# First projections of a three-block decoder: pairs of weight tiles by seven products instead of eight

## The chip, the cores and the metric

The kernel runs on one core of a Trainium2 chip. The metric is the device time of one execution in microseconds. The kernel before was timed three times: 2856.89, 2852.45 and 2854.75 us, median 2854.75.

## The reference, cut to what matters

The model is one block with three mixers side by side (window attention, RG-LRU, RWKV-7) and then two blocks with mixture-of-experts layers. Everything here happens at the very start of the first block, in the projection that makes the inputs of its three mixers:

```
D_MODEL = 1024; SEQ = 1024
proj = jnp.einsum("bsd,de->bse", x, w_in[l])                       # (1024 x 1024) @ (1024 x 2880), float32
q, k, v, g_a, x_b, g_b, c_cols, g_c = jnp.split(proj, split_idx, axis=-1)
y_a = _swa_sinks(q, k, v, attn_sinks[l])
y_b = _rg_lru(x_b, conv_w, conv_b, lru_wa, lru_ba, lru_wx, lru_bx, lru_lambda)   # conv, two sigmoid gates, scan
y_c, v_own = _rwkv7(c_cols, mu, w0, w2, a0, a2, k_k, k_a, r_k, gn_w, gn_b, vres) # token shift, tanh, sigmoids, state scan
y = jnp.concatenate([y_a * silu(g_a), y_b * silu(g_b), y_c * silu(g_c)], axis=-1)
```

## The kernel before, in words

`front` is the first phase of the program. It makes `proj` transposed: a tile is 128 output features (partitions) by 1024 tokens. `xT` holds x transposed, eight rows of 128 features by 1024 tokens (512 KB each). A tile's weights are 512 KB, loaded into one of two slots of `wbuf`. A tile is 16 matmuls of the source: two halves of 512 tokens, each a sum over eight rows of x (line 290). In float32 one matmul of the source shows as two instructions in the trace, so a tile is 32 instructions. `ORDER` is the order of the 20 tiles: two for the RG-LRU input (XB), one with the low-rank columns (WA), receptance (R), key (CK) and value (CV) of RWKV, two gates, four for the queries, one for the keys (K), four gates. Two more gate tiles (`LATE`) are made in the next phase. The attention values come with the tokens on the partitions and so are a separate group, `value_products` (line 270), 64 matmuls of 128 columns just ahead of the last tile.

The order of the work is written out by hand for each engine. TensorE goes through the tiles and puts six groups of `small` matmuls (line 245, four of the source each, 8 instructions) between them: two gate products of the RG-LRU, two low-rank products with only 32 rows, two sums over heads. ScalarE takes each tile out of PSUM in one piece (`evacuate`, line 299, the gates through Silu) and does the sigmoids, exponentials and roots of the mixers' inputs between them. VectorE does the convolution, the token shifts (`shift`, line 386), two scans, one reciprocal of 128x2048 (line 449) and products with it. SyncE loads tile m into a slot when tile m-2 is done. GpSimd issues the small loads, then makes masks, and has nothing more to do in this phase. The phase ends with a barrier of all engines. `acc` has four PSUM banks for the tiles, `aux` four for the small groups and the values.

The same way of seven products that the change brings in is already used two phases later, in `first_out` (`fo`, line 994): there GpSimd makes sums of operands (lines 1091 to 1096), TensorE runs groups of four matmuls (8 instructions, line 1110) and VectorE adds each product to its place (lines 1194 and 1201). Matrix shapes per group are the same: 128x128 weights by 128x512.

Of the kernel before, what the change touches and what calls it, by code (L numbers as in the profile page):

```python
# [11 lines left out]
P = 128  # L12
# [84 lines left out]
def col(v):  # L97
# [6 lines left out]
ORDER = [XB_T, XB_T + 1, WA_T, R_T, R_T + 1, CK_T, CK_T + 1, CV_T, CV_T + 1, G_T + 4, G_T + 5,  # L104
         Q_T, Q_T + 1, Q_T + 2, Q_T + 3, K_T, G_T, G_T + 1, G_T + 2, G_T + 3]
LATE = [G_T + 6, G_T + 7]
FRONT_TILES = len(ORDER)
K_AT = ORDER.index(K_T) + 1
GATE_AT = ORDER.index(G_T + 5) + 1


def in_tile(D, tile):
    return D["w_in_t"][tile - (tile > KS_T)]
# [22 lines left out]

def front(nc, D, proj, values, kkb, bb, dlt, wc, vec, win, ck):
# [5 lines left out]
    with Phase(nc, "fr") as ph:  # L143
        xT = win.xT
        wbuf = ph.sb("w", [P, 2, KT, P])
# [4 lines left out]
        keep = proj[:, KS_T]  # L150
        ones2 = ph.sb("ones2", [P, P])
# [7 lines left out]
        acc = ph.ps("acc", [P, 2, 2, 512])  # L159
# [4 lines left out]
        rr, kx, vv = (proj[:, m:m + TL] for m in (R_T, CK_T, CV_T))  # L164
        wv_loaded, loaded, vec_loaded = ph.sem("wv_loaded"), ph.sem("loaded"), ph.sem("vec_loaded")
        x_loaded = [ph.sem(f"x{k}_loaded") for k in range(KT)]
        w_loaded = [ph.sem("w0_loaded"), ph.sem("w1_loaded")]
        (done, evac, aux_done, aux_free, v_own, a_own, zeroed, conv_done, low_ready, tanh_low, sig_done, decay_done,
         tanh_done, root_in, root_done, logs_done, sq_ready, norm_done, cum_done, bonus_in, exp_done) = (ph.sem(n) for n in (
             "done", "evac", "aux_done", "aux_free", "v_own", "a_own", "zeroed", "conv_done", "low_ready", "tanh_low",  # L170
             "sig_done", "decay_done", "tanh_done", "root_in", "root_done", "logs_done", "sq_ready", "norm_done",
             "cum_done", "bonus_in", "exp_done"))
# [4 lines left out]

        with nc.Block() as block:

            @block.sync  # L180
            def _(sp):
                sp.dma_start(wbuf[:, 0], in_tile(D, ORDER[0])).then_inc(w_loaded[0], 16)
                for k in range(KT):
                    sp.dma_start(xT[:, k], D["xT"][:, k]).then_inc(x_loaded[k], 16)
                sp.dma_start(wbuf[:, 1], in_tile(D, ORDER[1])).then_inc(w_loaded[1], 16)
                for m in range(2, FRONT_TILES):

                    sp.wait_ge(done, m - 1)
                    sp.dma_start(wbuf[:, m % 2], in_tile(D, ORDER[m])).then_inc(w_loaded[m % 2], 16)
                    if m == FRONT_TILES - 1:  # L190

                        sp.wait_ge(evac, K_AT)
                        sp.wait_ge(cum_done, 1)
                        for h in range(2):
                            sp.dma_start(proj[HALF * h:HALF * h + HALF, KS_T],
                                         proj[HALF - HALF * h:P - HALF * h, K_T]).then_inc(turned_k, 16)
                for n, tile in enumerate(LATE):
                    sp.dma_start(win.wg[n], in_tile(D, tile)).then_inc(late_loaded, 16)
                sp.dma_start(win.sinks[:], D["attn_sinks"].partition_broadcast(P)).then_inc(late_loaded, 16)
                sp.wait_ge(turned_k, 32)  # L200
                sp.wait_ge(late_loaded, 48)

            @block.gpsimd
            def _(pool):
                pool.dma_start(lvec[:], D["lru_vec"]).then_inc(vec_loaded, 16)
# [3 lines left out]
                pool.dma_start(w2a2[RANK:2 * RANK], D["rwkv_a2"]).then_inc(loaded, 16)  # L209
                pool.wait_ge(zeroed, 1)  # L210
# [5 lines left out]
                pool.dma_start(wv, D["w_v_t"]).then_inc(wv_loaded, 16)  # L216
                g = nc.gpsimd
# [13 lines left out]
                for n in range(4):  # L231
                    select(ck.masks[:, n], ALU.is_ge if n % 2 == 0 else ALU.is_gt, -1, 1, 0.0, HALF)
                select(ck.lowm[:], ALU.is_ge, -1, 1, 1.0, HALF)
# [6 lines left out]
                select(ck.lowm[0:HALF], ALU.is_ge, -1, 1, 1.0)  # L240

            @block.tensor
            def _(pe):
                mm = nc.tensor.matmul
                def small(n, weights, moving, *waits):

                    if n:
                        pe.wait_ge(aux_free, n)
                    for s, value in waits:
                        pe.wait_ge(s, value)  # L250
                    for t in range(TL):
                        for c in range(2):
                            last = mm(aux[:, t, c], weights(t), moving(t)[:, 512 * c:512 * c + 512], start=True, stop=True)
                    last.then_inc(aux_done, 1)

                def smalls(m):
                    if m == 4:
                        small(0, lambda t: wa[:, t], lambda t: xc[:, t], (conv_done, 1), (loaded, 16 * 12))
                    if m == 5:
                        small(1, lambda t: wx[:, t], lambda t: xc[:, t])  # L260
                    if m == 10:
                        small(2, lambda t: w2a2[0:RANK, P * t:P * t + P], lambda t: lo[0:RANK], (tanh_low, 1))
                    if m == 11:
                        small(3, lambda t: w2a2[RANK:2 * RANK, P * t:P * t + P], lambda t: lo[RANK:2 * RANK])
                    if m == 14:
                        small(4, lambda t: ones2[:], lambda t: dlt[:, t], (sq_ready, 1))
                    if m == 16:
                        small(5, lambda t: ones2[:], lambda t: dlt[:, t], (bonus_in, 1))

                def value_products():  # L270
                    pe.wait_ge(wv_loaded, 16)
                    pe.wait_ge(aux_free, 6)
                    for t in range(NB):
                        for k in range(KT):
                            last = mm(aux[:, 0, t // 4, P * (t % 4):P * (t % 4) + P], xT[:, k, P * t:P * t + P], wv[:, k],
                                      start=(k == 0), stop=(k == KT - 1))
                    last.then_inc(aux_done, 1)

                for m in range(FRONT_TILES):
                    if m == FRONT_TILES - 1:  # L280
                        value_products()
                    b = m % 2
                    pe.wait_ge(w_loaded[b], 16 * (m // 2 + 1))
                    if m >= 2:
                        pe.wait_ge(evac, m - 1)
                    for c in range(2):
                        for k in range(KT):
                            if m == 0 and c == 0:
                                pe.wait_ge(x_loaded[k], 16)
                            last = mm(acc[:, b, c], wbuf[:, b, k], xT[:, k, 512 * c:512 * c + 512],  # L290
                                      start=(k == 0), stop=(k == KT - 1))
                    last.then_inc(done, 1)
                    smalls(m)

            @block.scalar
            def _(act):
                a = Chain(act, a_own)

                def evacuate(m):
                    act.wait_ge(done, m + 1)  # L300
                    gate = ORDER[m] < GATE_TILES
                    nc.scalar.activation(proj[:, ORDER[m]], flat(acc[:, m % 2]),
                                         ACT.Silu if gate else ACT.Copy).then_inc(evac, 1)
# [4 lines left out]
                for m in range(5):  # L308
                    evacuate(m)
                for n, (out, bias) in enumerate(((rg, 5), (ig, 6))):  # L310
                    act.wait_ge(aux_done, n + 1)
                    for t in range(TL):
                        a.hold(nc.scalar.activation(out[:, t], flat(aux[:, t]), ACT.Sigmoid, bias=lvec[:, t, bias:bias + 1]))
                    a.wait()
                    act.sem_inc(aux_free, 1)
                    evacuate(5 + n)
# [3 lines left out]
                act.sem_inc(tanh_low, 1)  # L320
                act.wait_ge(decay_done, 1)
# [4 lines left out]
                evacuate(7)  # L326
# [3 lines left out]
                for m in range(8, 11):  # L330
                    evacuate(m)
                for n, (out, bias) in enumerate(((lw, 3), (aa, 4))):

                    act.wait_ge(logs_done, 1)
                    act.wait_ge(aux_done, n + 3)
                    for t in range(TL):
                        a.hold(nc.scalar.activation(out[:, t], flat(aux[:, t]), ACT.Sigmoid, bias=vec[:, t, bias:bias + 1]))
                    a.wait()
                    act.sem_inc(aux_free, 1)
# [3352 lines left out]
```

## Time and profile before

| | us |
|---|---|
| median of three runs | 2854.75 |
| span of the profiled execution | 2854.7 |
| TensorE busy | 2528.5 (89%) |
| VectorE busy | 1082.8 (38%) |
| ScalarE busy | 541.8 (19%) |
| GpSimd busy | 263.9 (9%) |
| line 290, the tiles of `front` | 282.0 in 640 instructions |
| last taking out of a tile in `front` starts at | 326.29 |

The span of the profiled execution equals the median of the timed runs to a tenth of a microsecond. The phase `front` is the first 328 us of it, some 11% of the whole. A matmul's duration in the trace (0.59 us) is modelled and overlaps the next one; what counts is the distance between starts.

### The profile page before, as it was taken

The page shows a single profiled execution, that of the slowest core. Times are in us where ns is not written, and L with a number is a line of the kernel's source. Part 1 is how long each engine was busy: PE and PEld are TensorE (multiplying, and loading weights), DVE is VectorE, ACT ScalarE, POOL GpSimd, SP SyncE. Part 2 cuts the span into 40 slices and gives each one's busy share as a digit, 9 for nine tenths or more (in the row PEclk, how much of TensorE's full clock was granted, in tenths as well). Part 3 has the DMA queues.
Part 4 walks back from the last instruction along what each step waited for, and adds up shares of the span by engine and source line. Part 5 has one row for each costly group of instructions (what it writes and reads, how often), then busy time and mean ns, then how long its engine had stood idle before and what let it go on. Part 6 is the DMA issues. An engine that isn't in the chain of part 4 may idle for free. (4 is left out here: it accounts for less than half of the span.)

```text
span 2854.7 us, 40447 instructions
## 1 busy us (share of the span) xinstructions
PE 2528.5 (89%) x16570; PEld 1628.1 (57%) x16570; DVE 1082.8 (38%) x2424; ACT 541.8 (19%) x1314; POOL 263.9 (9%) x299
## 2 busy tenths in 40 slices
PE   8999999998999999887877879999999988887882
PEld 3444559845888755555555545666665555555551
DVE  2325366767555555211111143554555431111114
ACT  0212255411000011111111132222321111111112
POOL 1000000130000130111111000000003111111100
PEclk9999999998999999999999989999999999899986
DMA  3010010040112135999999971000023399999997
GB/s 113 30 37 30 30 46 4 21 153 31 45 45 102 63 136 193 385 420 419 420 421 420 418 303 37 18 24 8 8 86 133 136 378 419 420 420 420 420 420 302
DMA packets 108157, 566.14 MB, mean 198 GB/s; under 512 B 21681, under 2 KB 21841, under 8 KB 56497
## 3 DMA queue, kind: packets, MB, share of 16 engines
q1 hardware_dynamic: 82784, 506.34, 44.1%
q0 software_dynamic: 20288, 39.32, 3.6%
q10 hardware_dynamic: 4896, 17.83, 1.5%
q8 instruction: 136, 2.23, 0.3%
q14 instruction: 53, 0.43, 0.0%
HBM read 529.06 MB, written 65.01 MB: 208 GB/s over the span
## 5 line engine op out<-in xcount | busy, mean ns | idle before, releaser
L2698 PE MATMUL ex__h_ps<-all__arena,ex__xT 128*64 128x256 f32 x3392 | 530.6, 418 | 164.6 <-DMA all__arena<-in_w_gate 104.6
L2698 PEld LDWEIGHTS ex__h_ps<-all__arena,ex__xT 128*64 128x64 f32 x3392 | 341.0, 151 | 336.6 <-issue 222.0
L290 PE MATMUL fr__acc<-X__xT,fr__w 128*128 128x512 f32 x640 | 282.0, 601 | 9.2 <-DMA X__xT<-in_xT 9.2
L2741 DVE COPY ex__ysb<-ex__y_ps 128x512 f32<-128x512 f32 x64 | 44.3, 691 | 628.7 <-PE ex__y_ps L2718 628.3
L290 PEld LDWEIGHTS fr__acc<-X__xT,fr__w 128*128 128x128 f32 x640 | 122.2, 192 | 167.4 <-issue 158.1
L2698 PE MATMUL ex__h_ps<-mo__wx,ex__xT 128*64 128x256 f32 x704 | 180.2, 415 | 0.0
L2718 PE MATMUL ex__y_ps<-b__w,ex__hT 128*64 128x512 f32 x672 | 152.2, 592 | 0.9 <-ACT ex__hT L2735 0.9
L2059 PE MATMUL cm__acc<-all__arena,cw__w 128*128 128x260 f32 x576 | 136.0, 386 | 2.3 <-PEq L84 2.3
L2059 PE MATMUL cm__acc<-all__arena,cm__sums 128*128 128x260 f32 x576 | 135.2, 385 | 0.0
L2862 POOL DMA_INDIRECT b__rows<-s_hn,mo__queue x60 | 60.6, 1011 | 761.9 <-PE ex__x_ps L2691 761.9
L2059 PEld LDWEIGHTS cm__acc<-all__arena,cw__w 128*128 128x128 f32 x576 | 110.4, 192 | 19.8 <-issue 2.7
L2059 PEld LDWEIGHTS cm__acc<-all__arena,cm__sums 128*128 128x128 f32 x576 | 110.3, 192 | 17.3
L2729 ACT ACTIVATE ex__sg<-ex__h_ps 128x256 f32<-128x256 f32 x64 | 24.6, 384 | 418.0 <-PE ex__h_ps L2698 418.0
L2698 PEld LDWEIGHTS ex__h_ps<-mo__wx,ex__xT 128*64 128x64 f32 x704 | 103.6, 150 | 0.0
L2732 DVE TENSOR_TENSOR ex__hs<-ex__sg,ex__h_ps 128x256 f32<-128x256 f32 x64 | 27.0, 421 | 187.2 <-PE ex__h_ps L2698 187.2
L2718 PEld LDWEIGHTS ex__y_ps<-b__w,ex__hT 128*64 128x64 f32 x672 | 54.2, 137 | 72.9 <-issue 67.3
L2723 ACT COPY ex__xT<-ex__x_ps 128x512 f32<-128x512 f32 x64 | 37.5, 586 | 275.7 <-PE ex__x_ps L2691 275.7
L1600 PE MATMUL pb__acc<-b__w,all__arena 128*128 128x512 f32 x192 | 87.9, 603 | 1.8 <-PEq L84 1.8
L2425 PE MATMUL hd__o<-all__arena 128*128 128x128 f32 x704 | 85.6, 278 | 3.6 <-ACT all__arena L2482 3.6
L2425 PEld LDWEIGHTS hd__o<-all__arena 128*128 128x128 f32 x704 | 81.7, 192 | 6.4 <-ACT all__arena L2482 6.4
L2691 PE MATMUL ex__x_ps<-mo__ident,b__rows 128*128 128x128 f32 x512 | 75.5, 291 | 9.5 <-PEq L84 9.5
L2691 PEld LDWEIGHTS ex__x_ps<-mo__ident,b__rows 128*128 128x128 f32 x512 | 63.0, 195 | 35.0 <-issue 35.0
(514 smaller groups left out, 3989.7 us busy)
## 6 DMA issues: line engine op xcount, KB each, us to landing
all__arena<-in_w_gate SPq DMA_DIRECT2D x106, 1024.0 KB, 27.8
all__arena<-in_w_up SPq DMA_DIRECT2D x106, 1024.0 KB, 27.6
b__w<-in_w_down SPq DMA_DIRECT2D x84, 1024.0 KB, 28.6
all__arena<-in_w_down SPq DMA_DIRECT2D x22, 1024.0 KB, 26.4
mo__wx<-in_w_gate SPq DMA_DIRECT2D x22, 1024.0 KB, 28.4
mo__wx<-in_w_up SPq DMA_DIRECT2D x22, 1024.0 KB, 29.1
mo__wx<-in_w_down SPq DMA_DIRECT2D x22, 1024.0 KB, 29.7
all__arena<-s_ys SPq DMA_DIRECT2D x16, 1024.0 KB, 8.6
```

What stands on the lines that cost most here:

```text
L290: last = mm(acc[:, b, c], wbuf[:, b, k], xT[:, k, 512 * c:512 * c + 512], start=(k == 0), stop=(k == KT - 1))
L1600: last = mm(acc[:, bank], weight[:, k], moving[:, k], start=(first and k == 0), stop=(last_here and k == HK - 1), skip_group_check=not first)
L2059: last = nc.tensor.matmul(bank(u, x), weight(k), moving(k, c), start=(k == 0), stop=(k == HK - 1))
L2425: last = mm(o_ps[:, h, 0:P], vv[:, s, h], pT[:, h, a], start=(a == 0), stop=(a == len(tiles) - 1))
L2691: last = nc.tensor.transpose(x_ps[:, k // 4, P * (k % 4):P * (k % 4) + P], xe[:, b, k::KT], ident[:])
L2698: last = nc.tensor.matmul(h_ps[half, c, DE * b:DE * b + DE], xT[:, b, k, half], slots[n][:, c, k], start=(k == 0), stop=(k == KT - 1))
L2718: last = nc.tensor.matmul(y_ps[half, c], hT[:, b, k, half], slots[n][:, k, 512 * c:512 * c + 512], start=(k == 0), stop=(k == 1))
L2723: return nc.scalar.copy(xT[:, b, 0:4].rearrange("p k q -> p (k q)"), x_ps[:, 0])
L2729: return nc.scalar.activation(sg[:, b], h_ps[:, 0, DE * b:DE * b + DE], ACT.Silu)
L2732: return nc.vector.tensor_tensor(hs[:, b], sg[:, b], h_ps[:, 1, DE * b:DE * b + DE], ALU.mult)
L2741: return nc.vector.tensor_copy(ysb[:, b, 512:], y_ps[:, 1])
L2862: g.indirect_dma_start(xe[:, p % 2], None, hn_dram[:, :], bass.IndirectOffsetOnAxis(ap=queue[:, 0, p:p + 1], axis=0), bounds_check=T - 1, ...
```

## The change

Eight pairs of tiles (16 of the 20) are made by Strassen's seven products in Winograd's form. With a pair's weights cut into four pieces of 128 outputs by 512 features (A11, A12 of the first tile, A21, A22 of the second) and x cut into four quarters (512 features by 512 tokens), the pair is seven products of four matmuls (28) instead of eight (32). Four sums of weights are made per pair on GpSimd, four sums of x once on VectorE. Products that share a sum are added in PSUM: P6 goes on top of P1, P7 on top of both, P4 on top of all three, and ScalarE copies the bank out after each (`e_1`, `u`, `w`, `c_21`); P3 goes on top of P5. VectorE adds P2, P5 and P5+P3 to the copied halves (`c_11`, `c_22`, `c_12`). So each piece is taken out in halves of 512 tokens. The four tiles that are left (`SINGLE_TILES`) are made as before, by halves. The values' products come first, row by row of x as it lands, into eight PSUM banks. The weights are loaded in pieces of 256 KB into six slots. Silu on the two gate tiles of a pair is one instruction on SBUF. The mixers' steps keep their instructions but stand in a new order around the pairs.

The diff, cut to its core:

```diff
+PAIR_TILES = [(XB_T, XB_T + 1), (WA_T, K_T), (R_T, R_T + 1), (CK_T, CK_T + 1), (CV_T, CV_T + 1), (G_T + 4, G_T + 5),
+              (Q_T, Q_T + 1), (Q_T + 2, Q_T + 3)]
+SINGLE_TILES = [G_T, G_T + 1, G_T + 2, G_T + 3]
@@ sync @@
+                sp.dma_start(wv, D["w_v_t"]).then_inc(wv_loaded, 16)
                 for k in range(KT):
                     sp.dma_start(xT[:, k], D["xT"][:, k]).then_inc(x_loaded[k], 16)
+                    if k == 5:
+                        load(0, A11)
+                for which in (A21, A22, A12):
+                    load(0, which)
+                load(1, A11)
+                load(1, A12)
+                for n in range(1, NPT + 2):
+                    if n <= NPT:
+                        sp.wait_ge(product, p_at(n - 1, "P6"))
+                        sp.wait_ge(s_made, 4 * (n - 1) + S4)
+                        load(n, A21)
+                        sp.wait_ge(product, p_at(n - 1, "P7"))
+                        load(n, A22)
...
@@ gpsimd @@
+                def weight_sums(n):
+                    a11, a12, a21, a22 = (piece(n, w) for w in range(4))
+                    pool.wait_ge(w_loaded[slots[n][A21]], 16 * uses(n, A21))
+                    pool.wait_ge(w_loaded[slots[n][A22]], 16 * uses(n, A22))
+                    if n:
+                        pool.wait_ge(product, p_at(n - 1, "P5"))
+                    tt(s1[:], a21, a22, ALU.add).then_inc(s_made, 1)
...
+                    tt(a21, a11, a21, ALU.subtract).then_inc(s_made, 1)
+                    pool.wait_ge(s_made, 4 * n + S3)
+                    pool.wait_ge(product, p_at(n, "P1"))
+                    tt(a11, s1[:], a11, ALU.subtract).then_inc(s_made, 1)
+                    pool.wait_ge(s_made, 4 * n + S2)
+                    pool.wait_ge(product, p_at(n, "P2"))
+                    tt(a12, a12, a11, ALU.subtract).then_inc(s_made, 1)
@@ tensor @@
+                def product_of(bank, weight, moving, first):
+                    for k in range(HKT):
+                        last = mm(acc[:, bank], weight[:, k], moving(k), start=(first and k == 0), stop=(k == HKT - 1),
+                                  skip_group_check=not first)
+                    last.then_inc(product, 1)
+                def p_6(n):
+                    pe.wait_ge(taken, t_at(n, "E1"))
+                    pe.wait_ge(s_made, 4 * n + S2)
...
+                def p_5(n):
+                    if n:
+                        pe.wait_ge(added, a_at(n - 1, "C12"))
+                    pe.wait_ge(s_made, 4 * n + S1)
...
+                def p_7(n):
+                    pe.wait_ge(taken, t_at(n, "U"))
+                    pe.wait_ge(s_made, 4 * n + S3)
...
+                value_products()
+                p_1(0)
+                for n in range(NPT):
+                    p_2(n); p_6(n); p_5(n); p_7(n)      # small(0) at n = 1, small(2) at n = 3 behind p_7
+                    p_1(n + 1)                          # single_half(0, 0) behind the last pair
+                    p_4(n)                              # small(1) at 1, small(3) at 3, small(4) at 4, small(5) at 6
+                    p_3(n)
@@ scalar, around the pairs 5 and 6 @@
+                e_1(6)
+                c_21(5)
+                act.wait_ge(added, a_at(GATE_P, "C12"))
+                act.wait_ge(taken, t_at(GATE_P, "C21"))
+                nc.scalar.activation(proj[:, G_T + 4:G_T + 6], proj[:, G_T + 4:G_T + 6], ACT.Silu).then_inc(gated, 1)
+                u(6)
+                w(6)
@@ vector, pair 5 @@
+                c_11(5)
+                c_22(5)
+                dve.wait_ge(norm_done, 1)
+                v(V.reciprocal(dlt[:], dlt[:]))
+                v(V.tensor_tensor(kkb[:], kkb[:], dlt[:], ALU.mult))
+                v(V.tensor_tensor(bb[:], kkb[:], aa[:], ALU.mult))
+                c_12(5)
```

(The loop of TensorE and the comments in it are set in short form here.)

## Rows read from the trace of the kernel before

**Rows 1.** Waits of TensorE, 0 to 330 us: total us, times, longest.
```profile
PE fr__acc L290 <- DMA X__xT<-in_xT: 9.2, 7, 6.2
```
**Rows 2.** By stretch: length; PE, PEld, DVE, ACT, POOL; clock; DMA.
```profile
178.00:180.00 2.00, 2.00 (x3) 0.68 (x2) 0.00 (x0) 0.43 (x1) 0.00 (x0) 0.50 0.00 0
...
590.00:600.00 10.00, 10.00 (x25) 4.44 (x24) 6.14 (x11) 0.97 (x2) 3.18 (x2) 1.00 0.00 0
```
**Rows 3.** Timeline of TensorE in `front`: start, length, line, tiles, form, count.
```profile
84.50 13.90 PE L290 MATMUL fr__acc<-X__xT,fr__w 128*128 128x512 f32 x32
...
98.23 3.60 PE L253 MATMUL fr__aux<-fr__cum,fr__wx 128*128 128x512 f32 x8
...
170.42 4.50 PE L253 MATMUL fr__aux<-all__arena,fr__w2a 32*128 32x512 f32 x8
...
174.85 16.54 PE L290 MATMUL fr__acc<-X__xT,fr__w 128*128 128x512 f32 x32
...
191.33 3.69 PE L253 MATMUL fr__aux<-all__arena,fr__w2a 32*128 32x512 f32 x8
...
298.06 14.45 PE L275 MATMUL fr__aux<-all__arena,X__xT 128*128 128x128 f32 x128
...
312.35 13.90 PE L290 MATMUL fr__acc<-X__xT,fr__w 128*128 128x512 f32 x32
```
**Rows 4.** Timeline of the start, TensorE, as x lands.
```profile
6.18 3.52 PE L290 MATMUL fr__acc<-X__xT,fr__w 128*128 128x512 f32 x4 [6.18 <-DMA X__xT<-in_xT]
...
18.30 62.92 PE L290 MATMUL fr__acc<-X__xT,fr__w 128*128 128x512 f32 x146 [0.16 <-DMA X__xT<-in_xT]
```
**Rows 5.** DMA issues in `front`: tile, queue, count, size, median us to landing.
```profile
fr__w<-in_w_in_t SPq DMA_DIRECT2D x20, 512.0 KB, 3.4
```
**Rows 6.** Timeline of `first_out`, TensorE, products of 8 instructions.
```profile
593.06 1.88 PE L1110 MATMUL fo__acc<-all__arena,b__w 128*128 128x512 f32 x4
...
594.78 1.88 PE L1110 MATMUL fo__acc<-fo__late,b__w 128*128 128x512 f32 x4
...
596.49 5.31 PE L1110 MATMUL fo__acc<-all__arena 128*128 128x512 f32 x12
```
**Rows 7.** Timeline, taking 128x512 out of PSUM: ScalarE's copy, VectorE's addition.
```profile
342.19 0.59 ACT L593 COPY all__arena<-swa__f 128x512 f32<-128x512 f32 x1 [0.88 <-PE swa__f L550]
...
589.57 0.69 DVE L1201 TENSOR_TENSOR fo__xb<-fo__acc,fo__xb 128x512 f32<-128x512 f32 x1
```
**Rows 8.** Timeline of `first_out`, sums on GpSimd and VectorE side by side.
```profile
566.10 1.26 POOL L1091 TENSOR_TENSOR b__w<-all__arena 128x512 f32<-128x512 f32 x1 [18.41 <-POOLq L84]
...
566.30 3.22 DVE L1179 TENSOR_TENSOR b__w<-all__arena 128x2048 f32<-128x2048 f32 x1 [1.28 <-PEq L84]
...
567.45 3.20 POOL L1093 TENSOR_TENSOR b__w<-b__w,all__arena 128x512 f32<-128x512 f32 x1
...
581.53 3.86 POOL L1096 TENSOR_TENSOR b__rows<-all__arena,b__rows 128x512 f32<-128x512 f32 x1
```
**Rows 9.** Timeline of `front`: VectorE's convolution, reciprocal and product, ScalarE's 128x2048.
```profile
41.97 7.50 DVE L382 SCALAR_TENSOR_TENSOR fr__cum<-all__arena,fr__lvec,fr__cum 128x1023 f32<-128x1023 f32 x6
...
242.01 12.95 DVE L449 RECIPROCAL V__bonus<-V__bonus 128x2048 f32<-128x2048 f32 x1 [20.73 <-ACTq L347]
...
255.00 2.29 DVE L450 TENSOR_TENSOR V__kkb<-V__kkb,V__bonus 128x2048 f32<-128x2048 f32 x1
...
268.40 1.28 ACT L352 ACT_TABLE_LOAD   x1
...
269.69 1.91 ACT L352 ACTIVATE fr__aa<-fr__cum 128x2048 f32<-128x2048 f32 x1
```
**Rows 10.** Timeline at the end of `front`: the last tile taken out.
```profile
326.29 1.02 ACT L302 ACTIVATE all__arena<-fr__acc 128x1024 f32<-128x1024 f32 x1 [27.00 <-PE fr__acc L290]
```
**Rows 11.** Timeline of TensorE behind waits: a short one, and a long one.
```profile
1501.36 3.67 PE L2698 MATMUL ex__h_ps<-all__arena,ex__xT 128*64 128x256 f32 x32 [1.58 <-DMA all__arena<-in_w_gate]
...
1517.66 5.36 PE L2698 MATMUL ex__h_ps<-all__arena,ex__xT 128*64 128x256 f32 x32 [4.43 <-DMA all__arena<-in_w_gate]
```

More of the change, by code:

```diff
@@ L176, in flat, with p_at, t_at, a_at @@
             return x.rearrange("p a b -> p (a b)")
+        def p_at(n, which):
+            order = {"P1": 7 * n - 1, "P2": 7 * n + 2, "P6": 7 * n + 3, "P5": 7 * n + 4, "P7": 7 * n + 5, "P4": 7 * n + 7,
+                     "P3": 7 * n + 8}
+            if n == 0:
+                order["P1"] = 1
+            if n == NPT - 1:
+                order["P4"], order["P3"] = 7 * n + 6, 7 * n + 7
+            return order[which]
+        def t_at(n, which):
+            order = {"E1": 4 * n if n else 1, "U": 4 * n + 2, "W": 4 * n + 3, "C21": 4 * n + 5 - (n == NPT - 1)}
+            return order[which]
+        def a_at(n, which):
+            return 3 * n + {"C11": 1, "C22": 2, "C12": 3}[which]
+        S1, S3, S2, S4 = range(1, 5)
         with nc.Block() as block:
@@ L240, in _ @@
                 select(ck.lowm[0:HALF], ALU.is_ge, -1, 1, 1.0)
+                for n in range(3, NPT):
+                    weight_sums(n)
             @block.tensor
@@ L254, in small @@
                     last.then_inc(aux_done, 1)
[L256 to L268, printed above, removed]
@@ new lines, in value_products @@
+                    for k in range(KT):
+                        pe.wait_ge(x_loaded[k], 16)
+                        for t in range(NB):
+                            bank = acc[:, t, 0:P] if t < 4 else aux[:, (t - 4) // 2, t % 2, 0:P]
+                            last = mm(bank, xT[:, k, P * t:P * t + P], wv[:, k], start=(k == 0), stop=(k == KT - 1))
+                            if k == KT - 1 and t % 4 == 3:
+                                last.then_inc(values_done, 1)
+                b11 = lambda k: xT[:, k, low]
@@ new lines, in p_3, with single_half @@
+                def p_3(n):
+                    pe.wait_ge(added, a_at(n, "C22"))
+                    pe.wait_ge(s_made, 4 * n + S4)
+                    product_of(B, piece(n, A12), b22, False)
+                def single_half(g, c):
+                    n, m = NPT + g // 2, g % 2
+                    bank = (g % 2, (C, B)[g % 2])[c]
+                    if c == 0:
+                        for which in (2 * m, 2 * m + 1):
+                            weight_here(n, which)
+                    if g == 0 and c == 1:
+                        pe.wait_ge(added, a_at(NPT - 1, "C11"))
+                    if g == 1:
+                        if c == 0:
+                            pe.wait_ge(taken, t_at(NPT - 1, "C21"))
+                        else:
+                            pe.wait_ge(added, a_at(NPT - 1, "C12"))
+                    if g >= 2:
+                        pe.wait_ge(evac, 2 * (g - 2) + c + 1)
+                    for k in range(KT):
+                        last = mm(acc[:, bank], piece(n, 2 * m + k // HKT)[:, k % HKT], xT[:, k, 512 * c:512 * c + 512],
+                                  start=(k == 0), stop=(k == KT - 1))
+                    last.then_inc(single, 1)
@@ L297, in _, with take, e_1, u @@
                 a = Chain(act, a_own)
[L299 to L303, printed above, removed]
+                def take(out, bank, n, made_by):
+                    act.wait_ge(product, p_at(n, made_by))
+                    nc.scalar.copy(out, acc[:, bank]).then_inc(taken, 1)
+                def e_1(n):
+                    take(proj[:, PAIR_TILES[n][0], low], n % 2, n, "P1")
+                def u(n):
+                    take(proj[:, PAIR_TILES[n][0], high], n % 2, n, "P6")
+                def w(n):
+                    take(proj[:, PAIR_TILES[n][1], high], n % 2, n, "P7")
+                def c_21(n):
+                    take(proj[:, PAIR_TILES[n][1], low], n % 2, n, "P4")
+                def sigmoid(n, out, biases, bias):
+                    act.wait_ge(aux_done, n + 1)
+                    for t in range(TL):
+                        a.hold(nc.scalar.activation(out[:, t], flat(aux[:, t]), ACT.Sigmoid, bias=biases[:, t, bias:bias + 1]))
+                    a.wait()
+                    act.sem_inc(aux_free, 1)
                 act.wait_ge(vec_loaded, 16)
@@ L307, in _ @@
                 a(nc.scalar.activation(sp8[:, :, 1:2], sp8[:, :, 0:1], ACT.Ln, bias=1.0))
[L308 to L316, printed above, removed]
+                act.wait_ge(values_done, 1)
+                nc.scalar.copy(values[:, 0:4], acc[:, :, 0:P]).then_inc(values_out, 1)
+                act.wait_ge(values_done, 2)
+                nc.scalar.copy(values[:, 4:8].rearrange("p (a b) c -> p a b c", a=2), aux[:, :, :, 0:P]).then_inc(values_out, 1)
+                e_1(0)
+                u(0)
+                w(0)
+                e_1(1)
+                c_21(0)
+                u(1)
+                w(1)
+                sigmoid(0, rg, lvec, 5)
+                e_1(2)
+                c_21(1)
+                sigmoid(1, ig, lvec, 6)
                 act.sem_inc(sig_done, 1)
```

310 lines of the change are left out of this document (217 added, 93 removed).

## The prediction

> **What bounds the kernel now.** I read the waits of TensorE first: in the whole of `front` it waits only for x, 9.2 us in seven waits, the last ending at 18.30 [rows 1, 4]. From there to the last tile it never stops, so this phase costs what TensorE has to issue, and no other engine counts unless it is made late. Then the timeline gives the price of an instruction. From 84.50 to 98.23 there are 32 instructions: 0.4291 us each, 3.43 for a group of 8 [rows 3]. The values' products take 14.29 us from 298.06 to 312.35 for 128 instructions, 0.1116 each [rows 3].
>
> A check of these prices: 14 of the 640 tile instructions (two for each of the seven rows of x ahead of the last) start before 18.30; after it come 626 and 48 of the small groups, 674 x 0.4291 = 289.2, and 14.3 for the values, so 321.8. The last tile is taken out from 326.29 [rows 10]. Of the 4.5 us between, 3.75 lie in one place: from 170.42 to 174.85 a group takes 4.43 instead of 3.43, and the tile behind it, to 191.33, 16.48 instead of 13.73 [rows 3]. The granted clock is 0.50 there, the 1.2 GHz level [rows 2]. It fell behind the low-rank group, whose matmuls fill 32 rows, with no idle time; behind the second such group at 191.33 it did not fall [rows 3]. About 0.8 is left for the last matmul's drain and the handover.
>
> **The change, part by part.**
>
> *Products.* Eight pairs lose four matmuls of the source each, 8 instructions: 64 x 0.4291 = 27.5 us less. What is left behind the start: 56 products, 6 small groups and 16 groups of the four single tiles, 78 x 3.432 = 267.7 us. A product begins with two or three waits. Whether such a border costs anything is seen in `first_out`, which has the same groups: from 593.06 to 594.78 to 596.49 four instructions take 1.72, as inside a tile [rows 6]. I take nothing; the upper end would be the 0.16 by which a modelled duration exceeds the distance, 62 times 10 us, but I see no gap in those rows.
>
> *Values first.* They need 16 instructions per row of x, 1.79 us, against landings that ended at 18.30 for eight rows. The first 4 instructions of the run took 3.52 us, half speed [rows 4]. So I give the first row of x half speed: 6.18 + 3.57 + 7 x 1.79 = 22.3, and take 22.2 as the end of the values. Bounds: 20.5 at full speed throughout, 24.0 with two rows at half speed. x lands no later: one 512 KB load stands ahead of it as before, 256 KB are put in behind the sixth row, and the values' weights no longer come beside it from the other queue. P1 of pair 0 needs the first four value banks taken out (0.6 us, [rows 7]); those are complete 0.9 us before the values end. Taken with the first tile's head start that is lost, this part gains 14.3 - (22.2 - 18.3) = 10.4, less the 14 early instructions (6.0 us), which now come later: 4.4 net.
>
> *Sum.* 22.2 + 267.7 + 0.8 = 290.7. The clock's dip I keep, 3.75: the same 32-row groups stand there, 0 and 7.5 are the bounds. Now the waits.
>
> *Take-outs by ScalarE.* P7 may start when the copy of P6 is out, and P5 (3.43 us) lies between; a copy is 0.59 [rows 7], some 0.8 with handovers. P4 has P1 of the next pair between. Hidden, if nothing stands ahead in the queue. Pair by pair I walked the two queues: Tanh and the two 128x2048 instructions of pair 2 fit (5.1 us with a table load [rows 9], in a window of 10.3). The exception is pair 6, below.
>
> *Additions by VectorE.* 24 at 0.69 [rows 7], and the sums of x (four of 128x512 as early as x lands, four more, then two of 128x2048 at 2.29 [rows 9]). The last is due when P4 of pair 0 starts, 20 us after the values. C12 of a pair is due 6.87 us behind P3 (P2 and P6 of the next lie between). The convolution (six instructions 7.50 [rows 9], two more under 1 each) starts about 28 us after the values end and the first small group wants it at 41.2: 4 us to spare.
>
> *Weight sums.* The last piece of a pair's weights is issued when P7 of the pair before ends; a 512 KB load takes 3.4 us to land [rows 5], 256 KB no more. P6 is due 13.7 us behind P7. Three GpSimd sums stand between: 1.26 each alone, 3.86 at worst in the trace [rows 8], so 3.8 to 11.6 in 10.3. I take hidden; the bound is 1.3 in each of the pairs 2, 5, 6 and 7 where no small group widens the window, 5 us. That they hinder VectorE is seen at 566.30: its 128x2048 sum takes 3.22 beside a GpSimd sum that had started 0.20 before, 0.93 over 2.29, about what was left of it; the next on GpSimd, from 567.45, lasts 3.20, until just after VectorE is done [rows 8]. The Trainium skill, "SBUF — State Buffer", section "Who interferes with whom", has it so: a VectorE instruction with two SBUF inputs and a GpSimd one that reads SBUF take a shared port in turns, the second waiting in full. The trace agrees.
>
> *The reciprocal.* Between C22 and C12 of pair 5 VectorE has the reciprocal (12.95) and two products (2.33 each with their gap) [rows 9]. Put E at the end of P3 of pair 5. P7 ended at E - 10.3; its copy and C22 are done at E - 8.8. Reciprocal to E + 4.15; the S4 sum of pair 6 on GpSimd starts behind P2 at E + 3.5 and holds the next product up by 0.65; both products to E + 9.5; C12 to E + 10.2. P5 of pair 6 was due at E + 6.87: a stall of 3.4. Before, no tile waited for the same work, from 242.01 on. Then ScalarE: the Silu of the gate pair waits for that C12, with a table load of 1.28 and 1.91 of its own [rows 9], and the copy of P6 of pair 6 is queued behind it: out at E + 14.1, where P7 was due at E + 13.7. With handovers 0.5. Together 3.9 us lost. The bound below is 2.5 (no port wait, an earlier Silu), the one above 6.5.
>
> *The clock after that stall.* Behind a wait of 4.43 us 32 instructions took 5.36 against 3.67 behind one of 1.58 [rows 11]: 1.7 lost. A wait of 3.4 lies between; I take 0 and keep 1.7 as a bound.
>
> *The end.* The last take-out is 128x512, about 0.6 for 1.02 [rows 10]: 0.4 less. The late loads and the turned key tile go out 27 us before the last matmul and land under it.
>
> **The sum.** 290.7 + 3.75 + 3.9 = 298.35 against 326.29, so 27.9, and 0.4: 28.3 us less. All later phases start behind the barrier of this one, their loads too, so it should carry through. The profiled span is 2854.7 and the median 2854.75: 2826.4 us. With the bounds (values -1.7 to +1.8, dip -3.75 to +3.75, stall -1.4 to +2.6, weight sums up to 5, clock up to 1.7), which will not all fall on one side, its own range is 2820 to 2834.
>
> **Rivals.**
>
> *The weight sums set the pace.* Should loads land later or each sum meet a VectorE instruction of two inputs, 1.26 + 2.29 = 3.55 each, three are 10.7 in 10.3, and landings of 4 to 5 us add a microsecond or two in every pair: 7 x 1.5 = 10 us, 2837. Against it: a sum alone takes 1.26, and VectorE is idle for well over half of this phase, so that few sums meet it. Chance 6%.
>
> *The clock oscillates.* The products go round four banks with a wait ahead of each. If TensorE lost the full clock once per pair as it did at 170.42, that is 7 more dips of 3.0 to 3.75: 21 to 26 us, 2850. Against it: in `first_out` ten microseconds of just such products and waits run at 1.00 [rows 2]. Chance 3%. The Trainium skill, "TensorE: Matmul & The Clock Gate", section "A second HAM failure mode: psum-queue depth-cycling", tells of such swings where matmul groups go round PSUM banks; by the row of `first_out` they do not come with these groups.
>
> *Queue order in every pair: slower than before.* VectorE and ScalarE are strict queues, and each pair now needs seven handovers in them. What happens at the reciprocal would have to happen in all seven borders: from 4.1 us a pair (28.3 / 7 on top) the kernel is no faster. With 3.9 and the 1.7 of the clock behind each, 7 x 5.6 = 39 us: 2866. For it: the shares of VectorE's steps were put between the take-outs, 2 to 9 us long; against it: none but the reciprocal is longer than its window by the rows. Chance 4%.
>
> *It meets less waiting than I count*, the dip stays away or the reciprocal is covered: 2820 to 2822. Chance 12%, inside the range.
>
> The forecast has 75%. Faster by over 0.2% (5.7 us, about what a measurement of this kernel can tell from no change) holds in the forecast, the first rival and the last: 0.93. Within: half of the clock's rival and a part of the queue's, 0.03. Slower 0.04. The range for 8 in 10 is 2819 to 2836.
>
> **What would show it.** In the profile after: 576 instructions of 512 columns on the tiles' banks for 640, and distances of 0.4291; values ending near 22; TensorE waiting twice in pair 6, first for VectorE's C12 (about 3.4 us), then for ScalarE's copy (0.5), and nowhere else for more than half a microsecond; the last take-out of `front` starting near 298. Waits on GpSimd sums would show the first rival, a clock under 1.00 outside the 32-row groups the second, waits on `all__arena` from VectorE in most pairs the third.

## The result, and the profile after

The changed kernel takes 2829.47 us (median of four runs, 2826.04 to 2834.07) against 2853.6 for the kernel before (four runs): ratio 0.9914, 95% interval 0.9902 to 0.9925. That is 24.1 us less, where 28.3 were forecast, and 2829.5 us lies inside the range. Two more sets of timed runs of the unaltered changed kernel, told of below, gave 0.9899 (0.9883 to 0.9916) and 0.9894 (0.9877 to 0.991), with medians 2825.6 and 2826.2, beside 2856.27 and 2857.48 for the kernel before: 30.7 and 31.3 us less. The span of the profiled execution is 2824.3 us, its own time 2826.04, the lowest of the first four.

The phase `front` is where all of it lies. The waits of TensorE in its stretch, answering to [rows 1]; columns: who waits for what, us in total, times, longest:

```profile
PE fr__acc L363 <- DMA X__xT<-in_xT: 5.6, 1, 5.6
PE fr__acc L374 <- DVE all__arena L614: 3.2, 1, 3.2
```

The seven waits for rows of x have become one, for the first, and one wait for VectorE has come in. Its timeline at the start, at pair 3, at pair 6 and at the end, answering to [rows 3, 4 and 10]; columns: start, length, engine, line, tiles, form, count:

```profile
5.55 2.04 PE L363 MATMUL fr__acc<-all__arena,X__xT 128*128 128x128 f32 x8 [5.55 <-DMA X__xT<-in_xT]
...
9.10 1.50 PE L363 MATMUL fr__acc<-all__arena,X__xT 128*128 128x128 f32 x8
...
22.14 7.11 PE L374 MATMUL fr__acc<-X__xT,fr__w 128*128 128x512 f32 x16
29.08 3.60 PE L374 MATMUL fr__acc<-all__arena,fr__w 128*128 128x512 f32 x8
...
114.92 3.60 PE L374 MATMUL fr__acc<-fr__t,fr__w 128*128 128x512 f32 x8
118.44 3.69 PE L354 MATMUL fr__aux<-all__arena,fr__w2a 32*128 32x512 f32 x8
122.07 5.40 PE L374 MATMUL fr__acc<-X__xT,fr__w 128*128 128x512 f32 x8
127.30 3.60 PE L374 MATMUL fr__acc<-all__arena,fr__w 128*128 128x512 f32 x8
...
192.93 3.60 PE L374 MATMUL fr__acc<-all__arena,fr__w 128*128 128x512 f32 x8
199.75 5.40 PE L374 MATMUL fr__acc<-all__arena,fr__s 128*128 128x512 f32 x8 [3.23 <-DVE all__arena L614]
204.99 3.60 PE L374 MATMUL fr__acc<-fr__t,fr__w 128*128 128x512 f32 x8
...
249.62 48.23 PE L446 MATMUL fr__acc<-X__xT,fr__w 128*128 128x512 f32 x112
```

The values end where the first product starts, at 22.14. Products start 3.43 us apart, waits and all. Two products take 5.23 to 5.24 from start to start, 1.8 us too long: one behind the low-rank group at 118.44, one behind the wait at 196.4. The engines beside the second:

```profile
180.08 0.69 DVE L608 TENSOR_TENSOR all__arena<-fr__acc,all__arena 128x512 f32<-128x512 f32 x1 [5.52 <-ACT all__arena L487]
180.69 12.94 DVE L725 RECIPROCAL V__bonus<-V__bonus 128x2048 f32<-128x2048 f32 x1
...
186.93 1.28 ACT L571 ACT_TABLE_LOAD   x1
...
193.24 1.26 POOL L300 TENSOR_TENSOR fr__w<-fr__w 128x512 f32<-128x512 f32 x1 [6.91 <-PE fr__acc L374]
193.66 2.98 DVE L726 TENSOR_TENSOR V__kkb<-V__kkb,V__bonus 128x2048 f32<-128x2048 f32 x1
196.68 2.29 DVE L727 TENSOR_TENSOR V__bb<-V__kkb,fr__aa 128x2048 f32<-128x2048 f32 x1
199.01 0.69 DVE L614 TENSOR_TENSOR all__arena<-fr__acc,all__arena 128x512 f32<-128x512 f32 x1
...
199.73 1.91 ACT L571 ACTIVATE all__arena<-all__arena 128x2048 f32<-128x2048 f32 x1 [11.52 <-DVE all__arena L614]
```

Here stands C12 (line 614) behind the reciprocal and two products, and the first of these takes 2.98 instead of 2.29, because a sum on GpSimd (line 300) had begun 0.42 before it. The clock behind the low-rank group (first row) and behind the wait (second row); columns: stretch, length, busy time of PE, PEld, DVE, ACT, POOL, then the granted clock, DMA share, GB/s, as in [rows 2]:

```profile
124.00:126.00 2.00, 2.00 (x4) 0.71 (x3) 1.33 (x1) 1.64 (x2) 2.00 (x1) 0.50 0.00 0
...
202.00:204.00 2.00, 2.00 (x4) 0.97 (x3) 1.85 (x2) 0.12 (x1) 0.00 (x0) 0.50 0.00 0
```

The last take-out, and the first matmul of the next phase:

```profile
297.89 0.60 ACT L590 ACTIVATE all__arena<-fr__acc 128x512 f32<-128x512 f32 x1 [6.27 <-PE fr__acc L446]
...
299.54 0.71 PE L804 MATMUL swa__s<-all__arena 64*128 64x128 f32 x8 [1.69 <-PEq L84]
```

In the kernel before the last take-out started at 326.29 [rows 10] and the next phase at 328.29: `front` is 28.75 us shorter.

### The profile page after: what moved, and what is told of

It is laid out like the page before. It is cut to its first block and busy times, and to the rows that moved or that the text cites. A ratio compares the mean times of both kernels' runs of the same rounds, so it can differ in the third digit from the quotient of the medians.

```text
span 2824.3 us, 40528 instructions
## 1 busy us (share of the span) xinstructions
PE 2497.8 (88%) x16506; PEld 1619.4 (57%) x16506; DVE 1119.9 (40%) x2457; ACT 546.0 (19%) x1336; POOL 325.5 (12%) x330
## 5 line engine op out<-in xcount | busy, mean ns | idle before, releaser
L374 PE MATMUL fr__acc<-X__xT,fr__w 128*128 128x512 f32 x192 | 87.0, 603 | 0.0
```

The lines of the kernel that those rows point to most:

```text
L374: last = mm(acc[:, bank], weight[:, k], moving(k), start=(first and k == 0), stop=(k == HKT - 1), skip_group_check=not first)
```

## The experiments

**1. The changed kernel again.** No edit.

> The changed kernel again, unaltered. The profile had the phase `front` 28.8 us shorter, the timed runs gave 24. If the later phases carry the gain through and the rest is scatter of the runs, the ratio comes to 0.990 again (28 us), its profile shows the next phase starting at 299.5 and its later phases as long as before. If something later gives 4 us back in most runs, the ratio stays at 0.9914 and the profile of this run is likely to show a later phase that is some 4 us longer.

Measured: ratio 0.9899 (0.9883 to 0.9916), median 2825.6. The next phase starts at 298.5. What follows it, span less that start, lasts 2822.4 - 298.5 = 2523.9 us here, 2524.8 in the first profile, 2526.4 in the kernel before. Over the twelve profiles in which the whole computation is done it lies between 2523.9 and 2528.1, in no order with the length of `front`. The gain carries through; the 24 us of the first four runs, and the 31 us of the two repeats, are scatter of some microseconds around the 28.75 of the profile. That the next phase starts 1.0 us earlier here than in the first profile has two parts: the dip of the clock behind the low-rank group, 1.7 us, is absent (the product behind it runs from 122.73 to 126.27), and the values end 0.7 us later, at 22.80.

**2. One part alone: the values first.** The kernel before with (cut; ScalarE takes the values out here, as in the changed kernel)

```diff
+                sp.dma_start(wv, D["w_v_t"]).then_inc(wv_loaded, 16)      # ahead of x, was on GpSimd's queue
+                    for k in range(KT):                                   # ahead of the first tile
+                        pe.wait_ge(x_loaded[k], 16)
+                        for t in range(NB):
+                            bank = (acc if t < 4 else aux)[:, (t % 4) // 2, t % 2, 0:P]
...
-                    if m == FRONT_TILES - 1:
-                        value_products()
```

> The kernel before with one part of the change alone: the values' products first, as x lands; all 20 tiles by eight products. Theory: this part is worth 4.4 us (14.3 of values' products off the end, 3.9 and 6.0 back at the start), so `front` ends its last tile near 321.9 and the rest of the gain (about 24 us) belongs to the seven products. Rival: the values hide wholly under the load of x, 14.3 us, and the products are worth less than their count.

Measured: ratio 0.9986 (0.9977 to 0.9996), 4 us by the ratio and 5.2 by the medians; in its profile the next phase starts at 322.40, 5.9 us earlier than before.

```profile
180.47 3.70 PE L255 MATMUL fr__aux<-all__arena,fr__w2a 32*128 32x512 f32 x8
184.10 15.70 PE L294 MATMUL fr__acc<-X__xT,fr__w 128*128 128x512 f32 x32
199.72 3.69 PE L255 MATMUL fr__aux<-all__arena,fr__w2a 32*128 32x512 f32 x8
...
320.39 1.02 ACT L306 ACTIVATE all__arena<-fr__acc 128x1024 f32<-128x1024 f32 x1 [12.71 <-PE fr__acc L294]
```

The tile behind the low-rank group lost 15.62 - 13.73 = 1.9 us here, against 2.75 in the kernel before, and the group ahead of it 0.2 against 1.0; without this difference of 1.7 the part is worth 4.2 us, as worked out (4.4). The rival's 14 is out. So the seven products are worth the other 22.9 us of the 28.75: their count says 27.5, 3.4 and 1.8 are lost at pair 6, and the shorter last take-out gives 0.4. The products were not tried alone; their share is what is left over.

**3. C12 right behind the reciprocal.**

```diff
                 v(V.reciprocal(dlt[:], dlt[:]))
+                c_12(5)
                 v(V.tensor_tensor(kkb[:], kkb[:], dlt[:], ALU.mult))
                 v(V.tensor_tensor(bb[:], kkb[:], aa[:], ALU.mult))
-                c_12(5)
```

> In pair 5 VectorE adds C12 right behind the reciprocal, ahead of the two products of 128x2048. Theory: the reciprocal ends at 193.6, P3 is done at 189.5, so C12 is out near 194.4, before P5 of pair 6 is due (196.4): the wait of 3.2 us goes, and with it the half clock of 1.8 us behind it, 5.0 us in all; the last take-out of `front` starts near 292.8. Rival 1: the clock falls there for another reason (it would have fallen anyway): only 3.2 us. Rival 2: another wait (ScalarE's copy behind the Silu) takes its place: under 3 us.

Measured in its profile:

```profile
196.68 3.60 PE L374 MATMUL fr__acc<-all__arena,fr__s 128*128 128x512 f32 x8
200.11 3.60 PE L374 MATMUL fr__acc<-fr__t,fr__w 128*128 128x512 f32 x8
```

No wait, no half clock; the next phase starts at 294.7, 4.9 us earlier than in the first profile of the changed kernel, as the theory has it. Against its two repeats it is 3.8 and 3.5 us: the repeat of experiment 1 had no dip behind the low-rank group, and that of experiment 10 had the wait but no half clock behind it (shown there). Both rivals are out: P5 takes 3.43 us, and nothing waits in its place. Timed: 0.9888 (0.9871 to 0.9904), median 2823.19 beside 2825.6 of the changed kernel on the same chip. The intervals overlap; the gain is read from the profile.

**4. and 5. C12 between the two products, and later than both.**

```diff
                 v(V.tensor_tensor(kkb[:], kkb[:], dlt[:], ALU.mult))
+                c_12(5)
                 v(V.tensor_tensor(bb[:], kkb[:], aa[:], ALU.mult))
-                c_12(5)
```

> C12 of pair 5 stands between the two products of 128x2048. Theory: it is out at 197.4, the wait is 1.0 us instead of 3.2. If a wait has to be long before the clock falls, as it did behind 3.2 and not behind 1.6 in the kernel before, P5 of pair 6 takes 3.43 and all of `front` is 4.0 us shorter than in the changed kernel. Rival: any wait there costs the half clock: P5 takes 5.2, 2.2 us shorter.

```diff
                 v(V.tensor_tensor(bb[:], kkb[:], aa[:], ALU.mult))
-                c_12(5)
 
                 for t in range(TL):
                     v.hold(V.scalar_tensor_tensor(out=dlt[:, t], in0=rr[:, t], ...))
                 v.wait()
+                c_12(5)
```

> C12 of pair 5 stands behind the two 128x1024 steps as well (2.5 us more). Theory: the wait is 5.7 us, P5 at half clock again (+1.8): 2.5 us more than the changed kernel. Rival 1: the half clock lasts in proportion to the wait: over 3 us in P5. Rival 2: the copy behind the Silu now waits too and P7 stands: another 1 us.

Measured, P5 of pair 6, first in 4:

```profile
197.43 3.70 PE L374 MATMUL fr__acc<-all__arena,fr__s 128*128 128x512 f32 x8 [0.91 <-DVE all__arena L614]
200.97 3.60 PE L374 MATMUL fr__acc<-fr__t,fr__w 128*128 128x512 f32 x8
```

and in 5:

```profile
201.95 6.37 PE L374 MATMUL fr__acc<-all__arena,fr__s 128*128 128x512 f32 x8 [5.75 <-DVE all__arena L614]
208.16 3.60 PE L374 MATMUL fr__acc<-fr__t,fr__w 128*128 128x512 f32 x8
```

Behind a wait of 0.91 us the product takes 3.54, behind 5.75 us 6.21. So in these two profiles, one of each, the short wait cost itself (the next phase starts at 295.5, 4.0 us earlier than in the first profile of the changed kernel, as expected), the long one itself and 2.8 us of half clock, where I had expected 1.8. The first rival asked for over 3; 2.8 is too near to that to refuse it, but experiment 6 does, where 11.7 us cost less than 3.9. P7 did not wait (second rival out).

**6. Three times the weight sums.**

```diff
+                def more(n, at, a, b):                                    # ahead of S1, S3 and S2 of each pair
+                    for i in range(4):
+                        tt(junk[:], a[:, 0:2], b[:, 0:2], ALU.add).then_inc(junk_done, 1)
+                        pool.wait_ge(junk_done, 12 * n + 4 * at + i + 1)
```

> Ahead of each of the first three weight sums of a pair GpSimd makes four more of 128x256 into a scratch tile: three times the work, 12.2 us where it was 4.05 alone; result unchanged. Theory: the sums are hidden up to a slack that differs by pair. In the changed kernel the three are done at 46.4, 104.7, 186.3 and P6 is due at 53.1, 108.1, 192.9: so pairs 1, 3 and 6 come 1.5, 4.8 and 1.6 us late, the others hardly, about 8 us in all, plus 1.8 of half clock behind the wait of pair 3. Rival: the sums already lie on the path (each microsecond costs one): 8 pairs x 8.1 = 65 us.

Measured: 2872.33 us, the next phase at 346.1, 46.6 later than in the first profile of the changed kernel. Neither number holds. The waits of TensorE in `front`:

```profile
PE fr__acc L384 <- POOL fr__w L307: 32.2, 5, 11.7
PE fr__acc L384 <- issue: 7.1, 1, 7.1
```

and two of the chains on GpSimd, in pair 1 and in pair 2:

```profile
50.80 3.12 POOL L288 TENSOR_TENSOR fr__junk<-fr__w 128x256 f32<-128x256 f32 x4 [9.90 <-DMA fr__w<-in_w_in_t]
...
59.96 5.51 POOL L288 TENSOR_TENSOR fr__junk<-fr__s,fr__w 128x256 f32<-128x256 f32 x4
65.54 2.12 POOL L307 TENSOR_TENSOR fr__w<-fr__s,fr__w 128x512 f32<-128x512 f32 x1
...
84.05 3.14 POOL L288 TENSOR_TENSOR fr__junk<-fr__w 128x256 f32<-128x256 f32 x4 [10.93 <-DMA fr__w<-in_w_in_t]
...
96.44 1.27 POOL L307 TENSOR_TENSOR fr__w<-fr__s,fr__w 128x512 f32<-128x512 f32 x1
```

and, for comparison, the third sum of pair 0 in the changed kernel:

```profile
25.96 1.27 POOL L297 TENSOR_TENSOR fr__w<-fr__s,fr__w 128x512 f32<-128x512 f32 x1 [3.66 <-PE fr__acc L374]
```

Four small sums take 3.1 us and not 2.7, and where VectorE runs beside them the chain stretches: 16.9 us in pair 1 (50.80 to 67.66) where 12.2 were laid down, 22.3 in pair 3 (114.96 to 137.2). I had also left pair 0 out, whose P6 waits 7.1 us. Where pair 2 has its two small groups between, nothing waits although the chain is 13.7 us long. The six waits add up to 39.3 us, and each of the six products behind them ran in part at half clock: they took 5.2 to 6.2 us instead of 3.43, 13.9 us too long in all, with a granted clock of 0.56 to 0.67 on the average of each. Less the 7.0 us that the first profile of the changed kernel loses at pair 6 and behind the low-rank group, and this one does not, that is 46.2 of the 46.6. So the mechanism of the slack stands (six waits, none in pairs 2 and 4), and its size was read too kindly: GpSimd's time has to be counted with VectorE's beside it. In the changed kernel the three sums of pair 3 take 7.3 us, from 97.39 to 104.72, with P6 due at 108.05: a slack of 3.3 us. Only pair 0 has less: its third sum waits for P1 and is done at 27.23, 1.9 us ahead of P6 at 29.08.

**7. The low-rank groups with 128 rows.**

```diff
-        w2a2 = ph.sb("w2a2", [HALF, TL * P])
+        w2a2 = ph.sb("w2a2", [P, 2, TL * P])          # zeroed, then 32 rows of each half loaded
...
-  small(2, lambda t: w2a2[0:RANK, P * t:P * t + P], lambda t: lo[0:RANK], (tanh_low, 1))
+  small(2, lambda t: w2a2[:, 0, P * t:P * t + P], lambda t: proj[:, WA_T], (tanh_low, 1))     # small(3) likewise
```

> The two low-rank groups use 128 rows instead of 32: their weights stand in a zeroed tile of 128 rows, the moving operand is the whole tile of the low-rank columns. Result unchanged. Theory: the clock falls at 122 because of the 32-row group ahead of it, so it stays at 1.00 here and P1 of pair 4 takes 3.43 instead of 5.23: 2.0 us less in all. Rival: it falls there for another reason (time since the start, other engines' work) and the dip stays; 0 us.

Measured in its profile:

```profile
118.92 3.60 PE L354 MATMUL fr__aux<-all__arena,fr__w2a 128*128 128x512 f32 x8
122.35 3.60 PE L374 MATMUL fr__acc<-X__xT,fr__w 128*128 128x512 f32 x8
125.78 3.60 PE L374 MATMUL fr__acc<-all__arena,fr__w 128*128 128x512 f32 x8
```

The dip is gone, but it was also gone in the repeat of the changed kernel (experiment 1: 122.73, then 126.27), so this run alone proves nothing. Ratio 0.9899, the same as the repeat beside it. What the two 32-row groups cost apart from a dip is gone too. The seven groups from the start of P7 of pair 3 to P6 of pair 4 take 24.8 us in the repeat, which has no dip (115.58 to 140.39), and 24.0 here (115.48 to 139.52): 0.8 us for the two.

**8. 32 rows in three more groups** (the early C12 kept; part of the gate and bonus sums is left out, so only `front` is read).

```diff
-  small(0, lambda t: wa[:, t], lambda t: xc[:, t], ...)
+  small(0, lambda t: wa[0:RANK, t], lambda t: xc[0:RANK, t], ...)      # small(1) and small(5) likewise
```

> The kernel with the early C12, and three more of the small groups (both gate products of the RG-LRU and the bonus sum) use only their first 32 rows, so part of these sums is left out of the computation. Only `front` is read. Theory: a group with 32 rows can bring the half clock within a few microseconds of it, as it did at 122 in five profiles of seven; so in most of the three new places (behind about 67, 77 and 213 us) a product behind the group takes 1.8 to 2.8 us more than 3.43. Rival: rows have nothing to do with it; the three new places stay at 3.43 and only the place behind 122 may show it.

Measured: the products behind the three new groups stay at full speed, the old place dips.

```profile
64.17 3.70 PE L354 MATMUL fr__aux<-fr__cum,fr__wa 32*128 32x512 f32 x8
67.79 3.70 PE L374 MATMUL fr__acc<-X__xT,fr__w 128*128 128x512 f32 x8
...
78.48 7.13 PE L374 MATMUL fr__acc<-X__xT,fr__w 128*128 128x512 f32 x16
...
119.88 3.69 PE L354 MATMUL fr__aux<-all__arena,fr__w2a 32*128 32x512 f32 x8
123.50 5.40 PE L374 MATMUL fr__acc<-X__xT,fr__w 128*128 128x512 f32 x8
...
211.62 3.69 PE L354 MATMUL fr__aux<-V__bonus,fr__ones 32*128 32x512 f32 x8
215.25 7.13 PE L374 MATMUL fr__acc<-X__xT,fr__w 128*128 128x512 f32 x16
```

So my theory falls in its plain form. Counted over all thirteen profiles, the product or tile behind the first low-rank group lost 1.8 us or more in eight of ten with 32 rows, and in none of three with 128 rows. The rows seem to have a part in it; they do not suffice, and what else is special to that place (the operands' values, the tanh beside it) stays open.

**9. and 10. Both edits, twice, and the changed kernel a third time.**

> C12 of pair 5 right behind the reciprocal and the low-rank groups with 128 rows: no wait and no half clock left in `front` behind the start. Theory: the next phase starts at 298.5 - 4.9 - 0.9 = 292.7 (against 299.5 and 298.5 in the two profiles of the changed kernel), 35.6 us before the kernel before; ratio 0.9876. Rival: later phases give part back: ratio 0.989 or above as for the early C12 alone.

> The changed kernel once more, beside the version with both edits on the same chip: ratio 0.990 to 0.991; its next phase starts at 298.5 to 299.5.

> Both edits once more: `front` 6.8 to 7.8 us shorter than in the changed kernel in the profile (291.7 again) and a ratio lower by 0.0025 than that of the changed kernel on the same chip. Rival: the difference drowns in the scatter of the later phases.

Measured: with both edits the next phase starts at 291.7 and 292.7, against 299.5, 298.5 and 298.1 in the three profiles of the changed kernel: 5.4 to 7.8 us earlier. The one wait of TensorE in `front` of the first:

```profile
PE fr__acc L363 <- DMA X__xT<-in_xT: 5.6, 1, 5.6
```

In the third profile of the changed kernel, P5 of pair 6, and the clock (columns as above):

```profile
200.03 3.70 PE L374 MATMUL fr__acc<-all__arena,fr__s 128*128 128x512 f32 x8 [3.23 <-DVE all__arena L614]
203.57 3.60 PE L374 MATMUL fr__acc<-fr__t,fr__w 128*128 128x512 f32 x8
...
202.00:204.00 2.00, 2.00 (x7) 0.81 (x6) 1.85 (x2) 0.39 (x1) 0.00 (x0) 1.00 0.00 0
```

The wait is the same 3.23 us, yet the product behind it takes 3.54 at a granted clock of 1.00. So this wait brought the half clock in three profiles of four (the first, experiments 1 and 7, 1.8 us each) and not in the fourth. In the four profiles without the wait (experiments 3 and 8, and both edits twice) the product took 3.43 or 3.44 each time.

Timed: 2822.14 us, ratio 0.9894 (0.9877 to 0.991), and 2821.07 us, 0.9878 (0.9861 to 0.9894), where the changed kernel beside the second gave 2826.2 and 0.9894 (0.9877 to 0.991). The medians lie 5.1 us apart there, what the profile shows, but the intervals of the two ratios (0.9861 to 0.9894 and 0.9877 to 0.991) overlap. It has the lowest medians of the versions timed more than once; that it beats the changed kernel rests on the profiles more than on the ratios. The forecasts were met only in part. For the next phase 292.7 was forecast and 291.7 came, then 291.7 and 292.7 came. The ratios were to be 0.9876 and, the second time, 0.0025 below that of the changed kernel; they are 0.9894, which is the rival's value, and 0.0016 below. The changed kernel itself was to give 0.990 to 0.991 with a next phase at 298.5 to 299.5, and gave 0.9894 and 298.1.

## Why the prediction was right

Right side, and near in size: 28.3 us less were forecast, the profile has 28.75, and the three sets of timed runs 24.1, 30.7 and 31.3. The instructions are the forecast 576 (448 in the products, 128 in the single tiles), and TensorE waits once in pair 6, not twice. Term by term in the profile after, whose last take-out was forecast for 298.35 and came at 297.89:

*Products.* 78 groups at 3.43: as forecast. No border between two products costs anything that the rows show; the 32-row groups cost 0.8 us in all, counted with the dip below.

*Values first.* Forecast 22.2, measured 22.14. The first 16 instructions took 3.55 us, half speed, as the start of the kernel before had shown [rows 4]; the granted clock reads 1.00 in that stretch of either profile, so it is the pace that shows it and not the clock's row. The third group of 8 took 1.33, 0.4 more than laid down, and the rest 0.89; the first row of x was there at 5.55 and not at 6.18. So the agreement to 0.1 us is partly luck: over the twelve profiles with the values first they end between 21.4 and 22.9. Experiment 2 puts the part at 4.2 us net.

*The reciprocal.* Forecast 3.4 us of stall for P5 of pair 6, with GpSimd's S4 holding VectorE up by 0.65; measured 199.75 less 196.36, 3.4, and 0.69. Experiments 3 to 5 show that it is the order of VectorE's queue: with C12 in four places the wait is 0, 0.91, 3.23 and 5.75 us.

*ScalarE's copy behind the Silu.* Forecast 0.5, measured none. The step failed at the table load: I laid it behind the wait for C12, but it ran at 186.93, while ScalarE waited. The Silu then began at 199.73 and the copy was out at 202.12, ahead of the 203.2 at which P7 would have been due at full clock. The trace of the kernel before already had a table load that ran in such a wait, and I had not read it:

```profile
254.67 1.28 ACT L302 ACT_TABLE_LOAD   x1
267.36 1.02 ACT L302 ACTIVATE all__arena<-fr__acc 128x1024 f32<-128x1024 f32 x1 [11.41 <-PE fr__acc L290]
```

*The clock behind the stall.* I took 0 and kept 1.7 as a bound; measured 1.8. This is the term that was mis-sized, and it is not a fixed one either: behind this wait of 3.23 us the loss was 1.8 in three profiles of four and 0.1 in the fourth. Behind 0.91 us it was 0.1 (one profile), behind 5.75 us 2.8 (one profile). [Rows 11] already had 1.7 behind 4.43 us, and 3.4 was nearer to that than to 1.58.

*The dip behind the low-rank group.* Forecast 3.75 as before; measured 2.4: 22.99 us for the six groups from 118.44 to 141.43 instead of 20.59. In the repeat it was 0.7, which is what the 32-row groups cost with no dip at all (experiment 7). It is a term that comes and goes between runs of one kernel; the sum took the value of one profile, and its bounds of 0 and 7.5 held the rest.

*Sum.* Against the sum of terms the last three err by -0.5, +1.8 and -1.3 and cancel. The 0.46 that is left is the end: I allowed 0.8 between the last matmul and its taking out, but the 112 instructions from 249.62 run out at 297.68 by their count and the take-out starts at 297.89, 0.2 later. So `front` came out 28.75 us shorter for 28.3, and part of that agreement is luck.

*Carrying through.* Shown by experiment 1: the phases behind take 2524 to 2528 us whatever `front` does.

Of the rivals, the weight sums stay off the path, by 1.9 us in pair 0 and 3.3 us or more in the others. The clock did not swing, though products go round the banks all through: it reads 1.00 from 24 to 116, from 128 to 198 and from 206 to 300 us. The Trainium skill, "TensorE: Matmul & The Clock Gate", section "A second HAM failure mode: psum-queue depth-cycling", has such swings for another kernel with groups that go round PSUM banks; this trace has none for these. The queue order bit in one pair of eight, the one that the walk through the queues had found (28.3 / 7 is 4.0 and not 4.1 in that rival; nothing hangs on it). Less waiting than counted came only in parts, the absent dip of experiment 1 and the absent half clock of the third profile, and no median of the changed kernel lies below 2825.6.

## What to carry to other kernels

Where an engine is busy without a gap, count its instructions, and then walk the queues of the others, step by step, with the times of their instructions: the one long instruction between two handovers (here a reciprocal of 13 us) is the term that the count misses. Moving the handover two steps up in the queue gave back the wait of 3.4 us, and with it the half clock that stood behind it in three profiles of four. Time GpSimd's work with VectorE's beside it, not alone. A loss of clock seen in one profile may be absent in the next run of the same kernel; give it a range, and take several profiles before you call a wait its cause.

## What the runs showed of the hardware that was not expected

ScalarE loads the table for an instruction that still waits: at 186.93 for an instruction that started at 199.73, and in the kernel before at 254.67 for one at 267.36. The half clock behind a wait cost between 1.8 and 2.8 us for waits from 3.2 to 11.7 us, in ten cases of eleven; the eleventh is the third profile of the changed kernel, with 0.1. The loss does not grow with the wait: in experiment 6 the product behind 11.7 us took 5.57 instead of 3.43, that behind 3.9 us 6.10. And in eight of the ten profiles with 32 rows the product behind one certain group was 1.8 us or more too long with no idle time at all, the granted clock at 0.50 in part of it, but the products behind four other groups of the same form were not.
